# Turning sixteen heads' probabilities with VectorE and a DRAM scratch, and moving two attention stages forward in a two-block float32 network

## What is computed

```
# block 1, per layer: retention (4 heads), chunk attention (8 heads of 64),
# differential attention (4 heads), gates, merge, w_out, feed-forward
o_a = _retention(rq, rk, rv, rg, ret_norm_g)
...
# block 2, per layer: feed-forward, then the mixer, then feed-forward and ple
hm = mlstm_chunkwise(mq, mk, mv, ig, lf)        # 4 heads of 256, the "state attention"
hm = sigmoid(m_o) * head_rmsnorm(hm, m_out_norm)
ha = swa_gqa_sinks(aq, ak, av, a_sinks)         # 16 query heads of 64, 4 key/value heads
merged = sigmoid(g_m) * (hm @ w_branch_m) + sigmoid(g_a) * (ha @ w_branch_a)
h = h + merged @ w_out
```

## Time and profile before

| | us |
|---|---|
| median of 3 runs | 2307.66 (2304.9 to 2308.04) |
| profiled execution, its own time | 2307.95 |
| its span, first to last instruction | 2306.2 |
| TensorE busy (PE) | 2283.7, 99% |
| weight loads of TensorE (PEld) | 1906.6, 83% |
| VectorE busy (DVE) | 1527.7, 66% |
| ScalarE busy (ACT) | 1233.8, 53% |
| share of the chain that ended last: PE, DVE, DMA | 92%, 3%, 3% |

### The profile page before, as it was taken

One profiled execution on the slowest core, in us unless ns is written; L12 is line 12 of the kernel. 1 busy time (PEld: TensorE's weight loads), 2 busy tenths in 40 slices (PEclk: granted clock), 3 DMA queues, 4 the chain that ended last, 5 costly groups with the idle time before them and its releaser, 6 DMA issues.

```text
span 2306.2 us, 30120 instructions
## 1 busy us (share of the span) xinstructions
PE 2283.7 (99%) x11144; PEld 1906.6 (83%) x11144; DVE 1527.7 (66%) x2411; ACT 1233.8 (53%) x1890; POOL 128.6 (6%) x141
## 2 busy tenths in 40 slices
PE   9999999999999999999999999999999999999999
PEld 8887888888878888888878888888888888888887
DVE  6656786566567866576587765664766587657654
ACT  6555544445555454354467654554554478555543
POOL 3140000004300000000000000000000000000000
PEclk9999999999999999999999999999999999999999
DMA  8556568756475587577564444875677564456772
GB/s 336 199 192 238 190 220 290 228 185 214 156 267 186 172 287 242 180 256 248 189 230 157 157 155 165 265 241 195 219 244 238 178 215 156 150 171 209 233 235 89
DMA packets 179857, 483.08 MB, mean 209 GB/s; under 512 B 20480, under 2 KB 65152, under 8 KB 178688
## 3 DMA queue, kind: packets, MB, share of 16 engines
q1 hardware_dynamic: 179712, 481.16, 61.7%
HBM read 452.24 MB, written 28.84 MB: 209 GB/s over the span
## 4 chain that ended last, share of the span: by engine, by line
PE 92%; DVE 3%; DMA 3%; ACT 1%; SPq 1%; issue 1%; POOL 0%; DVEq 0%; ACTq 0%
PE bank L2104 27%; PE bank L2109 27%; PE bank L2108 27%; PE bank L2151 2%; PE bank L2091 2%; PE bank L2092 2%; PE bank L2093 2%; DMA raw<-in_weights 1%; DVE wl L1593 1%; PE bank L2240 1%; SPq L1181 1%; DMA rg<-moved 1%; DMA moved<-rv 0%; PE bank L2202 0%; PE bank L2225 0%
## 5 line engine op out<-in xcount | busy, mean ns | idle before, releaser
L1363 ACT ACTIVATE wh<-raw 128x1024 fp32r<-128x1024 f32 (+1 forms) x778 | 814.5, 1051 | 768.1 <-PE bank L2109 690.8
L1593 DVE TENSOR_TENSOR wl<-raw,wh 128x1024 fp32r<-128x1024 f32 (+1 forms) x778 | 927.8, 1223 | 282.9 <-ACT wh L1363 279.3
L2104 PE MATMUL bank<-wh,xh 128*128 128x512 f32 (+1 forms) x2102 | 826.8, 393 | 5.0 <-issue 3.9
L2109 PE MATMUL bank<-wh,xl 128*128 128x512 f32 (+1 forms) x2102 | 816.8, 389 | 0.0
L2108 PE MATMUL bank<-wl,xh 128*128 128x512 f32 (+1 forms) x2102 | 815.7, 388 | 0.0
L2104 PEld LDWEIGHTS bank<-wh,xh 128*128 128x128 f32 x2102 | 395.2, 188 | 87.0 <-issue 7.3
L2109 PEld LDWEIGHTS bank<-wh,xl 128*128 128x128 f32 x2102 | 394.9, 188 | 81.0
L2108 PEld LDWEIGHTS bank<-wl,xh 128*128 128x128 f32 x2102 | 395.5, 188 | 76.9
L2104 PE MATMUL bank<-wh,act_h 128*128 128x512 f32 x528 | 206.0, 390 | 0.0
L2109 PE MATMUL bank<-wh,act_l 128*128 128x512 f32 x512 | 199.4, 389 | 0.0
L2108 PE MATMUL bank<-wl,act_h 128*128 128x512 f32 x512 | 199.3, 389 | 0.0
(11 more groups left out here) (347 smaller groups left out, 2066.9 us busy)
## 6 DMA issues: line engine op xcount, KB each, us to landing
raw<-in_weights SPq DMA_DIRECT2D x760, 512.0 KB, 4.3
turn<-ffn_s SPq DMA_DIRECT2D x264, 64.0 KB, 2.8
ffn_a<-turn SPq DMA_DIRECT2D x66, 256.0 KB, 4.7
raw<-in_weights SPq DMA_DIRECT2D x16, 384.0 KB, 3.2
ln<-in_ln SPq DMA_DIRECT2D x4, 1024.0 KB, 6.8
moved<-merged SPq DMA_DIRECT2D x32, 128.0 KB, 3.5
merged<-moved SPq DMA_DIRECT2D x8, 512.0 KB, 7.0
bias<-in_bias SPq DMA_DIRECT2D x2, 1024.0 KB, 9.3
```

The source lines that it names most:

```text
L1363: act.activation(wh[:, u % NH, 0:used(u)], raw[:, u % NR, 0:used(u)], ACT.Copy).then_inc(hi_done, 1)
L1593: dve.tensor_tensor(wl[:, u % NR, 0:used(u)], raw[:, u % NR, 0:used(u)], wh[:, u % NH, 0:used(u)].bitcast(F32), ALU.subtract).then_inc(lo_ ...
L2104: pe.matmul(out, h, w_h, start=st.first and i == 0, stop=False)
L2109: last = pe.matmul(out, lo, w_h, start=False, stop=ends)
```

## The change

It does five things.

1. In block 2 a pair's probabilities are turned by `block`, `out`, `back` like the other tensors, with one VectorE transpose of 128 x 768, four DMAs of 96 KB out and one of 384 KB back. `aa_pv` waits for the DMA and reads its moving operand from the landed buffer as pieces of 32 columns that lie 192 columns apart. The pairs use three stage buffers in turn. The `probs_T` steps of these heads and their copies are gone. The two parts of a head in `Pn` change places.
2. `mo` is turned the same way, in two halves of 512 KB.
3. In block 2 the `out` and `back` of `ak`, `aq0` and `aq1` stand up to four units earlier, and the state attention (`m_rows` to `m_fin`) five units earlier.
4. In block 1 the retention's products, `ret_fin` and its `block`, `out` and `back` stand four to five units earlier, the differential attention two.
5. `weave` reads a place for each side step instead of a count of units between them.

```
-UNITS_AMONG_2 = "10000020101100011211002110001101011110011110401001111100100111101101000101020040102"
...
+PAIRS_AT = (6, 8, 12, 15, 19, 22, 26, 29)
+PAIR_STEPS = (("pv", 8), ("even", 2), ("s", 0), ("block", 3), ("out", 4), ("back", 6))
...
-    q["o"] = heads(p, "aa", AH // 2, scores, q["akv"])
+    done, evens = {}, {}
+    for _, _, what, pair in sorted((at + after, k, what, pair) for pair, at in enumerate(PAIRS_AT)
+                                   for k, (what, after) in enumerate(PAIR_STEPS)):
+        h = 2 * pair
+        if what == "s":
+            done[h] = scores(h)[1]
+        elif what == "even":
+            evens[pair] = p.count("even", 2)
+            p.add("even", h=h, of="aa", soft=done[h], m=p.count("shares"))
+        elif what == "block":
+            p.moved("block", f"pair{pair}", h=h, m=evens[pair])
+        elif what in ("out", "back"):
+            p.moved(what, f"pair{pair}", h=h)
...
-    p.add("load", name="gain_ple", t=tt[MH - 1])
-    t_m = split_rows("mo", "hm", KT, rows=p.cc["rows"])
+    for what in ("block", "out", "back", "halve"):
+        for r in range(R):
+            h_m = p.moved(what, f"mo{r}", rows=p.cc["rows"], dst="hm", tile=r)
...
+                    elif k == "block" and st.name.startswith("pair"):
+                        dve.wait_ge(evened, st.m)
+                        dve.transpose(stage[st.name].rearrange("p (q m n) -> p q m n", q=4, m=6),
...
+                        else:
+                            pe.wait_ge(moved_back[st.name], 16 * (st.l + 1))
...
+                            pairs = landed[st.name].rearrange("p (b m n) -> p m b n", b=4, m=6)
```

More of the change, by code:

```diff
@@ L168, in begin, with weave @@
         return kept
[L170 to L183, removed]
-        self.steps = before
[L185 to L191, removed]
+    def weave(self, before, dense, side, places):
+        assert len(places) == len(side), (len(places), len(side))
+        self.steps = before
+        left = sorted(zip(places, side), key=lambda pair: pair[0])
+        done = 0
+        for st in dense:
+            if st.kind == "unit":
+                while left and left[0][0] <= done:
+                    self.steps.append(left.pop(0)[1])
+                assert not any(sd.t is not None and sd.t == st.after_t for _, sd in left), st.u
+                assert not any(sd.kind == "o_split" and sd.o + 1 == st.after_o for _, sd in left), st.u
+                done += 1
+            self.steps.append(st)
+        self.steps += [sd for _, sd in left]
     def flip(self):
@@ L442, in plan_block1 @@
     for r in range(R):
-        h_a = p.moved("back", f"rg{r}", rows=p.cc["rows"], dst="oa", tile=r)
+        h_a = p.moved("halve", f"rg{r}", rows=p.cc["rows"], dst="oa", tile=r)
+    p.add("load", name="bm12", s=ret_s3, roped=roped)
+    p.add("load", name="ln1", roped=roped)
     for src in ("dq", "dk"):
         c_d = p.moved("out", src, roped=q[src + "_rope"].n)
-    for r in range(R):
-        h_a = p.moved("halve", f"rg{r}", rows=p.cc["rows"], dst="oa", tile=r)
     for src in ("dq", "dk"):
@@ L683, in plan_block2 @@
     p.add("m_narrow", c=c_log)
+    p.moved("back", "aq0")
+    p.moved("out", "aq1")
     p.add("p_split")
@@ L716, in plan_block2 @@
         p.add("a_sum", tile=r)
-    for what in ("out", "back", "copy"):
-        for name in ("ak", "aq0", "aq1"):
-            c_a = p.moved(what, name)
+    for name in ("ak", "aq0", "aq1"):
+        if name == "aq1":
+            p.moved("back", name)
+        c_a = p.moved("copy", name)
     p.add("m_log2")
@@ L743, in plan_block2 @@
     p.add("m_fin", rows=p.count("rows"), o=p.o - 1)
[L744 to L745 removed]
+    for what in ("block", "out", "back", "halve"):
+        for r in range(R):
+            h_m = p.moved(what, f"mo{r}", rows=p.cc["rows"], dst="hm", tile=r)
+        if what == "block":
+            p.add("load", name="gain_ple", t=tt[MH - 1])
     side = p.begin()
```

78 lines of the change are left out of this document (50 added, 28 removed), and 3 rows, old and new, of the table PLACES_2.

## The result

The changed kernel takes **2314.45 us** (median of 5 runs, 2314.09 to 2315.8), the kernel before in the same comparison 2307.39 (2302.83 to 2308.04). The ratio is 1.0037, with a 95% interval of 1.0024 to 1.0051: slower by 0.37%, where I had forecast 2297.4 and 0.45% faster. The profiled execution took 2315.64 us around a span of 2313.9.

The account below looks back on a forecast made before the run. TensorE was taken as the bound, busy 2283.7 of 2306.2 us. From 2307.95, gains of 24.6, less 12.4 for the pairs' gaps and 1.6 for the clock, gave 2297.4 us; forecast 2290 to 2304 (chance 0.58), range 2285 to 2307.

Parts of the forecast that it names:

- TensorE's work: Block 2: no turning of heads (10.3 us) and `mo` (3.5) on TensorE, less separate groups (2.4), saves 11.4 us.
- The 2.4 us for separate groups: Block 2: `aa_s` and `aa_pv` no longer side by side, so twelve more groups to enter and leave cost 2.4 us.
- rival C: Pairs' `aa_pv` in block 2: operand pieces halve TensorE's rate, adding 13 us, 2310, no change; chance 0.05.
- Block 1: Retention in block 1: the waits for `oa_l` and the low clock behind them go, saving 11.8 us.
- Rival D of the prediction: Block 1's gain doesn't come, as `da_s` or a ScalarE copy waits instead: 2309, no change; chance 0.07.
- The pairs' landings: Block 2: each pair's 384 KB way back lands in 5.4 us, bounds 4.7 and 6.9.
- Pair 0's gap: Ahead of the first `aa_pv` of each layer in block 2: a gap of 3.3 us, bounds 2.6 and 4.8.
- Rival A: Pairs in block 2: ways back land fast enough, pair 0 waits 1.0 us, the others nothing: 2285.4; chance 0.2.
- Pair 6: Block 2: its way back stands behind the load of `gain`; gap 2.3 us a layer, bounds 1.1 and 3.3.
- The whole stretch: Block 2: VectorE gets some 8 us on 116 of 170 and doesn't become the bound.
- one drop at 1.6: Clock behind the pairs' gaps in block 2: one more drop, costing 1.6 us, bounds 0 and 6.4.
- Rival B: Pairs in block 2: DMA rings slow the ways, all eight pairs of a layer wait: 2315; chance 0.1.

Follow-up runs that it names:

- e10: e9 with the state attention and `mo` placed as before the change: 2290.09 us, ratio 0.9944 to the kernel before.
- e2: The kernel before with only the change's part for block 1, block 2 untouched: 2296.91 us, ratio 0.9958.
- e4: e1 with the products of pairs 0, 3, 4 and 7 one unit later and pair 6's two later: 2313.14 us, ratio 1.0032.
- e1: The changed kernel with the load of `gain` four units later, behind the ways back of pairs 6 and 7: 2311.28 us, ratio 1.0030.
- e3: The changed kernel with pair 7's even, block, out, back and product each two units later: 2310.30 us, ratio 1.0017.
- e5: e4 with the state attention and the turning of `mo` put back as before the change: 2310.70 us, ratio 1.0027.
- e12: e10 with seven pairs' scalings (`even`) one or two units sooner, no longer directly ahead of the next pair's scores: 2307.53 us, ratio 1.0006.
- e8: e7 with scores and scalings of pairs 1, 2, 3, 6 and some steps of pairs 0 and 3 one or two units sooner: 2312.87 us, ratio 1.0033.
- e7: e4 with the state attention and `mo`'s steps two units later: 2308.28 us, ratio 1.0013.
- e9: e1 with the state attention one unit later and each pair's scalings directly ahead of the next pair's scores: 2291.68 us, ratio 0.9946.
- e6: The changed kernel's places, but each pair turned by TensorE again, without VectorE transposes or DMAs for the pairs: 2363.49 us, ratio 1.0247.
- e11: e9 with the state attention and `mo` at e7's places: 2298.90 us, ratio 0.9973.

## Why the prediction was wrong, by its own steps

**TensorE's work: 11.4 against 11.5, by luck.** The turned pieces in the stretch of layer 0, before and of the changed kernel (count, then busy, mean ns, idle):

```profile
L2151 PE MATMUL bank<-ident,Pn 128*128 128x128 f32 x60 | 9.5, 273 | 0.0
```

```profile
L2189 PE MATMUL bank<-ident,Pn 128*128 128x128 f32 x12 | 2.0, 272 | 0.0
```

By distances from start to start the 48 pieces took 4.15 us a layer, 8.3 in two, where I had 10.3 from one head, and the 16 of `mo` 1.58 a layer, 3.2 where I had 3.5. The 2.4 us for separate groups were nothing: scores take 6.83 us a layer in the kernel before and in e10. So the heads were 2 us too dear and the groups 2.4, and the two errors cancelled. The moving operand in pieces costs nothing either (6.4 us a layer in the kernel before and in e10), so rival C is out.

**Block 1: right, a little too high.** 9.7 us by e2's ratio (6.9 to 12.7), 11.8 forecast. The wait for `da_s` that I had ruled out is there, about 1 us in layer 0 (ScalarE's `kT`). Rival D of the prediction is out.

**The pairs' landings: sooner than forecast.** 384 KB landed in 4.5 us (median), where I had 5.4, and under my lower bound of 4.7:

```profile
merged<-moved SPq DMA_DIRECT2D x12, 384.0 KB, 4.5
```

Pair 0's gap was 1.5 and 1.9 us for 3.3, and `mo` was in time. Rival A (2285) took the landing for what decides; in e4, where nothing waits for a landing, the time is 2313.

**Pair 6: the step that failed.** The prediction says: "That unit ended at 1298.9 and `gain` was issued at 1302.12, 3.2 us later." The 3.2 us were read from the kernel before, where the gate of unit 434 stands ahead of the `even` of pairs 6 and 7, and carried into a list where both stand ahead of it. In the changed kernel pair 7's scalings end at 1299.98 and the gate follows at 1300.84. It was 11.0 us, the gap 8.3 for 2.3, so 12 us in two layers.

**The whole stretch: the same mistake, larger.** I costed the steps on ScalarE and VectorE only by their durations ("some 8 us on 116 of 170; it doesn't become the bound") and for what DMAs wait on them, and put at nothing, without a reason, what the new order does to their waits for each other. (For the two gaps ahead of unit 407 alone I said that the queue is unchanged, and these stayed at 2.0.) Neither engine is the bound, and yet ScalarE's waits for sums and maxima grew from 16 to 31 us from 1195 to 1340, and gates, banks and `a_rows` were late. That is the rest: 2.8 us in layer 0 ahead of units 429 and 431 (gaps of 1.81 and 1.31, less a step of 0.12 and 0.23), 2.4 in layer 1, and the clock, two windows of 10.2 us that cost 4.9 where I had one drop at 1.6, and one of 3.4 us more, behind unit 407 of layer 1. Pair 0 gave back 3.2. e1, e3, e4 and e5 take away one reader each and gain 1 to 4 us, hardly clear of noise. That the order of `even` and scores is worth this much, e12 against e10 shows, 14 to 17 us; how it runs on from ScalarE's waits to each wait of TensorE's in the changed kernel was not traced step by step.

**The chances.** C, D and half of B add up to 0.17 and not to 0.13, as that line has it.

**Rival B** had the right time (2315) for a wrong reason: one pair of eight waited much, and it didn't wait for the rings. Its own test, 1.5 us on average per pair, came out at 1.3 (20.6 over 16).

**The rule on turning.** The Trainium skill, "VectorE: DVE Perf Modes", Rules for kernel authors, would leave 128x128 turning on TensorE. The changed kernel seems to bear it out; e10 against e2 speaks the other way, with 3 to 7 us less by VectorE and the scratch once the order is right, though not clear of noise. What bears on the failure is the Trainium skill, "PSUM — Partial Sum Buffer", Engine vs sequencer instructions: "ScalarE/VectorE/GpSimdE queues are strict FIFO." The traces agree: in the changed kernel ScalarE stood 5.56 us ahead of one pair's exponentials (1252.77), and the `wh` behind them came at 1255.00.

## What to carry to other kernels

Where two engines work in order and hand things to each other, count the waits for hand-overs in each queue, not only the busy time: lay steps so that one wait covers the next (a pair's scalings directly ahead of the next pair's exponentials, while the other engine makes their maxima). A delay read from the kernel before (from a unit's end to its gate) can be carried over only if nothing new stands ahead of it in any of the queues on its way. And a gap that names a DMA may hide a second one of nearly its size: move the reader away before believing in the landing.

## What had not been expected of the hardware

Longer gaps mostly went with longer times at the lower clock: 8.3 us with 10.2 us, 5.6 in e4 with 6.8, 4.5 and 4.0 in the kernel before with 3.4 each. But gaps of 4.1 us went with 6.8 us in both layers of e12 and with 3.4 in both layers of e8. And the gap of 2.0 us ahead of unit 407, seen in both layers of every kernel, went with the lower level in both layers of the changed kernel, e7 and e9, in one layer of the kernel before and of e1 to e4, e6, e11 and e12, and in none of e5, e8 and e10. In e10 the profile shows 2.4 GHz from 5 us after the start to the end.
